# A decoder layer's expert stage: rows in four column quarters, transposed in 32x32 squares by VectorE, weights in 16 KB runs, row loads asked for by GpSimd

## What is computed

```python
mod = (cond @ ada_w[l] + ada_b[l])[:, None, :]
sh1, sc1, g1, sh2, sc2, g2 = jnp.split(mod, 6, axis=-1)
...
u = rms_norm(x, norm2_g[l]) * (1.0 + sc2) + sh2
x = x + g2 * grouped_moe(u, w_router, moe_w1[l], moe_w3[l], moe_w2[l])

def grouped_moe(u, w_router, w1, w3, w2):   # 16 experts, 2 of them for each token
    ...
    for e in range(N_EXPERTS):
        h = jax.nn.silu(xt @ w1[e]) * (xt @ w3[e])       # 1024 -> 512
        y = y + gate[:, e:e + 1] * (h @ w2[e])           # 512 -> 1024
```

## Time and profile before

| | us |
|---|---|
| median of 3 runs | 765.2 (763.77 to 767.42) |
| the profiled execution | 763.06 |
| its span, first to last instruction | 761.3 |
| PE busy | 619.2 (81%) |
| DVE busy | 325.2 (43%) |
| ACT busy | 253.6 (33%) |
| POOL busy | 78.2 (10%) |

### The profile page before, as it was taken

One profiled execution on the slowest core, in us unless ns is written; L12 is line 12 of the kernel. 1 busy time (PEld: TensorE's weight loads), 2 busy tenths in 40 slices (PEclk: granted clock), 3 DMA queues, 4 the chain that ended last, 5 costly groups with the idle time before them and its releaser, 6 DMA issues.

```text
span 761.3 us, 15584 instructions
## 1 busy us (share of the span) xinstructions
PE 619.2 (81%) x6207; PEld 371.4 (49%) x6211; DVE 325.2 (43%) x925; ACT 253.6 (33%) x611; POOL 78.2 (10%) x118
## 2 busy tenths in 40 slices
PE   0898999967599998799972288989999999999940
PEld 0544474654366666554462154545555555555520
DVE  3714828242578999822445021222222222222215
ACT  4200200132357668711230142434433433443410
POOL 5001000034100000000001200101001101100122
PEclk9998999989689999999965599999999999999985
DMA  8970957070799000092081659999999999999228
GB/s 323 379 299 10 404 194 274 2 232 0 234 302 250 17 2 1 1 335 107 0 320 46 218 174 352 362 360 363 369 360 361 370 362 362 363 374 355 59 53 309
DMA packets 81388, 176.25 MB, mean 231 GB/s; under 512 B 9410, under 2 KB 26378, under 8 KB 79306
## 3 DMA queue, kind: packets, MB, share of 16 engines
q1 hardware_dynamic: 68592, 152.90, 57.5%
q0 software_dynamic: 8384, 13.97, 5.4%
q10 hardware_dynamic: 4380, 8.94, 3.7%
HBM read 155.02 MB, written 20.71 MB: 231 GB/s over the span
## 4 chain that ended last, share of the span: by engine, by line
PE 27%; DMA 23%; DVE 2%; issue 2%; POOL 2%; ACTq 0%; ACT 0%; POOLq 0%
DMA featT<-expert_rows 21%; PE score L1534 9%; PE score L1454 7%; PE score L1543 4%; PE bank L1524 4%; PE score L1494 2%; DMA pool_sb<-expert_rows,idx 1%; POOL expert_rows L768 1%; POOL pool_sb L788 1%; DMA expert_rows<-pool_sb,idx 1%; DMA expert_rows<-featT 1%; PE bank L1549 0%; ACTq L664 0%; PE bank L1486 0%; PE bank L1402 0%
## 5 line engine op out<-in xcount | busy, mean ns | idle before, releaser
L1534 PE MATMUL score<-pool_sb,featT 128*32 128x256 f32 x2688 | 161.4, 384 | 23.4 <-DMA featT<-expert_rows 14.7
L1534 PEld LDWEIGHTS score<-pool_sb,featT 128*32 128x32 f32 x2688 | 86.4, 110 | 84.4 <-DMA featT<-expert_rows 29.9
L1250 PE MATMUL bank<-pool_sb,featT 128*128 128x512 f32 (+2 forms) x256 | 89.3, 511 | 5.8 <-DVE featT L843 2.6
L1190 DVE TENSOR_TENSOR featT<-featT,score 128x128 f32<-128x128 f32 x42 | 12.1, 288 | 186.2 <-ACT featT L675 186.2
L1543 PE MATMUL score<-pool_sb,featT 128*32 128x256 f32 x1344 | 82.8, 387 | 0.4 <-ACT featT L680 0.4
L1250 PEld LDWEIGHTS bank<-pool_sb,featT 128*128 128x128 f32 x256 | 50.0, 196 | 43.5 <-issue 35.8
L669 ACT ACTIVATE featT<-bank,mod_col 128x32 f32<-128x32 f32 x129 | 39.3, 374 | 61.5 <-PE bank L1524 61.5
L776 POOL DMA_DIRECT2D expert_rows<-featT x42 | 29.1, 692 | 280.2 <-DVE featT L1186 266.5
L1180 DVE TENSOR_SCALAR featT<-bank,mod_col 128x32 f32<-128x32 f32 x215 | 51.0, 303 | 15.1 <-PE bank L1524 15.1
L1454 PE MATMUL score<-pool_sb,featT 128*128 128x512 f32 x128 | 55.6, 594 | 0.0
L675 ACT ACT_TABLE_LOAD x42 | 53.9, 1283 | 0.8
(11 more groups left out here) (243 smaller groups left out, 688.0 us busy)
## 6 DMA issues: line engine op xcount, KB each, us to landing
pool_sb<-in_moe_w SPq DMA_DIRECT2D x48, 2048.0 KB, 21.2
pool_sb<-in_ada_w SPq DMA_DIRECT2D x16, 1024.0 KB, 7.4
expert_rows<-zeros_f SPq DMA_DIRECT2D x17, 512.0 KB, 6.2
featT<-expert_rows ACTq DMA_DIRECT2D x44, 128.0 KB, 5.5
expert_rows<-featT POOLq DMA_DIRECT2D x42, 128.0 KB, 7.1
pool_sb<-in_ada_w SPq DMA_DIRECT2D x8, 640.0 KB, 12.3
pool_sb<-in_w_out SPq DMA_DIRECT2D x4, 1024.0 KB, 16.7
pool_sb<-in_ada_w SPq DMA_DIRECT2D x8, 384.0 KB, 9.7
```

Source lines behind the costliest of these rows:

```text
L1250: m = nc.tensor.matmul(pj_bank(g, i)[:, 0:n], featT[:, k, i * P:(i + 1) * P], w_stage[:, g % 3, k, 0:n], start=(k == 0), stop=(k == KD - 1))
L1534: mm = nc.tensor.matmul(banks[0][h * BT:(h + 1) * BT, 0:2 * HB], xgT[:, k, :], exp_w13[slot][:, :, k, h * HB:(h + 1) * HB], start=(k == 0) ...
```

## The change

The reduction index is split otherwise. A row of 1024 columns is cut into four quarters of 256; quarter h lies on the 32 partitions from 32h on. After DVE has transposed each 32x32 square of the tile, partition p holds columns 8p to 8p+7 of all 32 rows. The weights are viewed as `(p k) n` to match, so that partition p takes eight consecutive rows of w1 and w3 (four of w2): one run of 16 KB for each partition. Scale and shift become whole tiles `scale2_part` and `shift2_part` in the quarter form, and are applied before the transpose. PE transposes nothing in the loop and ACT does Silu alone there. The loads of rows are issued by POOL, behind the store of an earlier block, into two tiles.

```diff
-        xg = blkbuf[0:BT, 0:D]
+        xg = [blk_view(DN) for _ in range(2)]
...
+            for h in range(NT):
+                sp.dma_start(scale2_part[h * BT:(h + 1) * BT, :], norm2_g[0:1, h * DN:(h + 1) * DN].broadcast_to([BT, DN])).then_inc(s_n2, 16)
...
-                             MOE_W[m][0, e].rearrange("(k p) n -> p k n", p=P)).then_inc(done, 16)
+                             MOE_W[m][0, e].rearrange("(p k) n -> p k n", p=P)).then_inc(done, 16)
...
-            sp.wait_ge(s_xg, 32)
+            sp.wait_ge(s_scat, 16 * 2 * TT)
             load_matrix(2, 0)
...
-            def block_of_rows(g):
+            def silu_of(g):
                 act.wait_ge(m_h1, g + 1)
                 nc.scalar.activation(silu, banks[0][:, 0:HB], ACT.Silu).then_inc(m_si, 1)
-                act.wait_ge(m_xt, g + 2)
-                xg_load(g + 2)
-                xg_T(g + 1)
-                act.wait_ge(m_ht, g + 1)
-                nc.scalar.activation(hT, banks[6][:, 0:P], ACT.Copy).then_inc(m_hT, 1)
...
+            def xg_load(g, n):
+                pool.dma_start(xg[n], xs[bass.ds(g * BT, BT), :].rearrange("r (h n) -> h r n", h=NT)).then_inc(s_xg[n], 16)
...
+            pool.wait_ge(s_scat, 16 * 2 * TT)
+            for g in range(5):
+                if g >= 2:
+                    pool.wait_ge(m_sc, g - 1)
+                xg_load(g, g % 2)
...
             with pool.Fori(0, pairs - 1) as m:
                 for n in range(2):
                     store_rows(y_sb[n], m * 2 + n, n)
+                    pool.wait_ge(m_sc, m * 2 + (n + 4))
+                    xg_load(m * 2 + (n + 5), 1 - n)
...
+            def rows_in(g, n):
+                dve.wait_ge(s_xg[n], g * 8 + (16 if n == 0 else 8))
...
+                nc.vector.tensor_tensor(xm, xg[n], scale2_part[:], ALU.mult).then_inc(m_sc, 1)
+                dve.wait_ge(m_sc, g + 1)
+                nc.vector.tensor_tensor(xm, xm, shift2_part[:], ALU.add).then_inc(m_mod, 1)
...
+                nc.vector.transpose(xgT, xm.rearrange("p (r k) -> p k r", k=KD)).then_inc(m_xT, 1)
+
+            def hmid_T(g):
+                dve.wait_ge(m_h, g + 1)
+                nc.vector.transpose(hT, hmid.rearrange("p (r k) -> p k r", k=NT)).then_inc(m_hT, 1)
...
+            def block_of_rows(g, n, y):
+                hidden(g)
+                dve.wait_ge(m_y, g)
+                hmid_T(g)
+                rows_out(y)
+                rows_in(g + 2, n)
...
-                        pe.wait_ge(s_xg, g * 16 + 32)
...
             def stage_of(g, slot, slot_before, uses):
                 pe.wait_ge(e_w13[slot], uses * 32)
+                pe.wait_ge(m_h, g)
                 inner(slot, g)
-                xg_T()
                 pe.wait_ge(e_w2[slot], uses * 16)
                 outer(g - 1, slot_before)
-                inner_T(g)
```

More of the change, by code:

```diff
@@ L78, in decoder_layer @@
         gate2_part = sb("gate2_part", [P, DN])
+        scale2_part = sb("scale2_part", [P, DN])
+        shift2_part = sb("shift2_part", [P, DN])
         gate1_row = sb("gate1_row", [P, D])
@@ L324, in decoder_layer @@
         s_scat = sem("s_scat")
-        s_xg = sem("s_xg")
+        s_n2 = sem("s_n2")
+        s_xg = [sem(f"s_xg{n}") for n in range(2)]
+        m_mod = sem("m_mod")
+        m_sc = sem("m_sc")
         m_h1 = sem("m_h1")
@@ L1519, in _, with inner @@
             m.then_inc(r_rank, 1)
[L1521 removed]
+            def inner(slot, g):
+                pe.wait_ge(m_xT, g + 1)
                 for k in range(KD):
[L1523 to L1532 removed]
                     for h in range(NT):
```

132 lines of the change are left out of this document (62 added, 70 removed).

## The result

The changed kernel is slower. Its time is 798.3 us (794.3 to 802.7) beside 764.5 us (762.3 to 767.4) for the kernel before in the same runs: a ratio of 1.043, 95% interval 1.039 to 1.047. The forecast was 735.5 us with a range of 720 to 752. The profiled execution has a span of 800.4 us, 39.1 us more than before.

The account below looks back on a forecast made before the run. Row-load latency plus transposes was taken to bound the blocks, weights close behind. Gain 30.2 us from weights at 18.3 us an expert, less 0.5 for the prologue, is 29.7: 763.06 becomes 733.4, plus 2.1 to the median, 735.5 us (720 to 752).

Parts of the forecast that it names:

- PE's turn of 5.5 us: Stage of the blocks: without its transposes PE needs 5.5 us for a block, against 7.07 us today.
- The cover of 1.87 us: PE's second product, 1.87 us, hides the DVE transpose, Silu and its product (0.8 to 1.6 us), at cost 0.
- The row loads at a cost of zero: Stage of the blocks: loads behind POOL's stores land in 11.7 us, under the 12.9 us allowed, so cost 0.
- two turns and some slack: Time allowed for a row load to land: 2 x turn + 1.9 us, 12.9 us at a turn of 5.5.
- 0.33 us for each KB of piece size: Growth of a POOL transfer's landing with weight piece size, from two stores; gives 11.7 us at 16 KB.
- The last rival but one: "Slower than before": store and load in POOL's queue both stretched, landing 17.2 us, turn 7.65 us, 787 us; chance 0.04.
- Larger pieces, 4 to 6% off: Expert weights in 16 KB pieces take 4 to 6% off 17.1 us, bringing an expert's pace to 18.3 us.
- PE will wait for weights next: Stage of the blocks: PE would need 14.4 us for an expert, weights give one in 18.3, waits from expert 6.
- that case, 702.5 us: Forecast's own case, weights setting the pace: last product ends at 702.5 us, today 732.7; gain 30.2 us, chance 0.55.
- What bounds before: Kernel before: row-load latency plus transposes, 7.07 us a turn, with weights close behind at 19.35 us for an expert.
- Start and end: +1.5 us ahead of the first product, mostly not counted since weights decide; prologue 0.5 us (0 to 1); end unchanged.
- The chance of 0.92 for faster: Whole kernel: chance of being faster by over 0.5% (3.8 us); same 0.04, slower 0.04.

Follow-up runs that it names:

- e4: Kernel before, with only the expert weights read in runs of 16 KB: 796.5 us.
- e9: Changed kernel with ACT asking for row loads, POOL for stores, both in column quarters, weights in 2 and 4 KB pieces: 739.7 us.
- e7: Changed kernel with ACT asking for row loads, POOL for stores, both in column quarters, weights in 8 KB pieces: 730.2 us.
- e6: Changed kernel, weights still in 16 KB, with ACT asking for row loads and POOL for stores, both in column quarters: 753.2 us.
- e1: Changed kernel with only the weights back in pieces of 2 and 4 KB: 775.0 us.
- e10: e7 with SP asking for w1 of expert 2 only when the first two blocks' rows are in: 726.4 us.
- e8: Kernel before, with only POOL's row stores split into four column-quarter transfers: 758.2 us.
- e5: Changed kernel, weights in 16 KB, row loads and stores both still on POOL but each split into four column quarters: 774.2 us.
- e3: Changed kernel, weights in 16 KB, with ACT instead of POOL asking for the unsplit row loads: 822.3 us.

## Why the prediction was wrong

1. **PE's turn of 5.5 us**: right, and slightly too high (5.19 us). DVE's transposes take 0.65 us for 256 columns and 0.41 us for 128, against an estimate of 0.42 for the first and bounds of 0.29 to 1.19. The cover of 1.87 us held.
2. **The row loads at a cost of zero**: this is the step that failed. Its form was wrong, not only its number. It asked whether a landing of 11.7 us fits into two turns and some slack. Measured is 16.7 us, and DVE waited 83.4 us for loads and 46.0 us for stores. A queue that serves two transfers of 6.1 us for each block is busy for 12 us of it, and no depth of the ring helps; the wait then grows until landings are 17 to 23 us. The number 11.7 came from 0.33 us for each KB of piece size, read from two stores. For one store the slope was not bad (e4: 11.1 us). Left out was that the store's twin stands in the same queue, and that the load in its new form has the store's long line of packets: on ACT's queue it had two on an engine and would have grown to 6.6 us only.
3. **The last rival but one** ("slower than before") named this mechanism: L = 17.2 us, a turn of 7.65 us, 787 us. Measured: 16.7 us, a mean turn of 325.1 / 42 = 7.74 us (blocks without weights beside them included), 798 us. That its 7.65 us comes so near is partly luck: single turns run from 5.2 to 12.5 us, and 7.7 is only their mean. It was given 0.04 because rows pass unhindered when SP's queue runs empty. They seem to, since the mean turn is 7.74 us and not 12, but that is a relief which sets in only after PE has waited. The chance was far too small: two measured stores and the order of POOL's queue spoke for this case, and only a relief that comes late spoke against it.
4. **Larger pieces, 4 to 6% off**: right in size. 392 to 412 GB/s from 2 and 4 KB to 8 KB (e9, e7), 5%; at 16 KB the fullest slice of e6 has 416. In the changed kernel it could not show, as the weights were not asked for in time.
5. **PE will wait for weights next**: right for the kernels in which rows are out of the way (e1, e7), not for this one. The end of that case, 702.5 us for the last product, was even too late: in e7 it ends at 702.9 us after a start 12.1 us later than before, in e10 at 692.6 after a start 1.7 us later.
6. **What bounds before**: the prediction took 362 GB/s and 19.35 us for an expert as the weights' own pace. e8 shows that part of it was made by the stores' form. I had not asked on how many engines a transfer of [4, 32, 256] lies.
7. **Start and end**: +1.5 us was forecast from the last scatter to the first product and was 6.0. The change lets the first weight matrix of expert 2 go with the first rows and not behind them; the prediction read this edit only for its good side, that weights are asked for earlier. e10 gave it back. For the prologue 0.5 us were taken (0 to 1 as ends); it costs 1.8 to 3.1 us. Where in that stretch it is lost was not followed further; eight records of the quarter matmuls take 0.64 us by themselves.
8. **A cost not in the sum**: PE's clock. In 15 of 42 blocks the first product took 5.0 to 6.6 us in place of 3.66 (starts and lengths in the timeline) because PE had waited just before it. Together that is 28 us of PE's time. How much of it reached the end is not shown; in the turn from 589.40 to 600.87 nothing did, as PE had ended both products by 596.5 and stood until the rows were there.

The chance of 0.92 for faster rested on step 2 alone. The change does hold the gain that was forecast: with the rows in quarters and their loads on ACT's queue it is 730 us in pieces of 8 KB (753 in 16 KB), and 726 us with the first rows put first.

## What to carry to other kernels

Before making one stream's pieces larger, count for every other transfer beside it how many packets stand in line on one engine, and multiply by the new packet's time (here 8 x 0.69 = 5.5 us for 6.1 to 6.2 measured; for e5's four it gave too little, 2.6 for 4.0 to 5.0); then add up all that share its queue and compare the sum with the turn, not the latency with the depth of the ring. A transfer whose slowest dimension is 4, as [4, 32, 256] here, is worth splitting along it (822 to 762 us by the loads alone), if the engine that issues it has nothing urgent behind the extra issues (0.3 to 0.6 us each here). A large load that used to start behind a small critical one, and now starts beside it, holds the small one up, even though it is asked for earlier (10.4 us in place of 4.9 to the first product).

## What the runs showed of the hardware

- One and the same view of 128 KB in 1 KB runs travels as packets of 4 KB in POOL's queue and of 1 KB in ACT's (e3), and split into quarters as 2 KB in POOL's (e5). Beside 16 KB pieces a form is the slower the more packets it has on one engine: 4.0 to 5.0 us of the queue with 4, 6.1 to 6.2 with 8, and by estimate 21 with 32; not in proportion, though.
- With rows spread, one core alone held 411 to 416 GB/s over nine slices of 18.3 us in a row (e7), where the kernel before had 362.
- The rate of all queues can fall to half for a microsecond at a busy share of 90% or more, once for each block (kernel before, and less deep in e8). No run settled why.
- A medium size was best: 8 KB pieces (730 us) beat 2 and 4 KB (740) by their rate, and 16 KB (753) by what they let pass.
